# HGRN head pipeline one iteration deeper, four results taken out of PSUM by ScalarE, and two weight loads issued earlier

## The reference, cut to what matters

```python
def _hgrn2_mixer(h, w_in, lower_bound, out_norm, w_out):
    proj = h @ w_in                                   # 1024 x 1024 @ 1024 x 4096
    q, f, i, g = jnp.split(proj, 4, axis=-1)
    log_f = logaddexp(log(lb), log1p(-lb) + log_sigmoid(f))
    k  = (1.0 - lb) * sigmoid(-f)
    qf = silu(q) * HGRN_HEAD_DIM ** -0.5
    # per head: S_t = diag(f_t) S_{t-1} + k_t v_t^T ; o_t = S_t^T q_t     (v = i)
    o = scan(qf, k, i, log_f)
    o = o * rsqrt(mean(o * o, -1) + eps)              # per head
    return (o * out_norm * silu(g)) @ w_out
...
# then: x + mix, RMS norm, squared-ReLU MLP (1024 -> 4096 -> 1024), norm;
# a second block with a convolution/retention mixer and the same kind of MLP; final norm.
```

## Time and profile before

| | |
|---|---|
| time, median of 3 runs | 2488.07 us (2487.45 to 2489.05) |
| the profiled execution's own time | 2485.64 us |
| its span, first to last instruction | 2483.5 us |
| PE busy | 2437.6 us, 98% |
| DVE busy | 1049.2 us, 42% |
| ACT busy | 417.3 us, 17% |
| POOL busy | 900.4 us, 36% |
| granted TensorE clock over the span | 0.997 |

### The profile page before, as it was taken

The page is one execution under the profiler, slowest core; times in us unless marked ns, Lnnn a source line. Parts: engine busy times, 40 slices in busy tenths (PEclk is TensorE's granted clock), DMA queues, the critical chain, the costliest instruction groups (busy, mean ns, idle before and its releaser), DMA issues.

```text
span 2483.5 us, 30216 instructions
## 1 busy us (share of the span) xinstructions
PE 2437.6 (98%) x11520; PEld 2029.4 (82%) x11520; DVE 1049.2 (42%) x1449; ACT 417.3 (17%) x691; POOL 900.4 (36%) x1020
## 2 busy tenths in 40 slices
PE   7999999999999999999999999999999999999998
PEld 6888888788888888888888888888888888888886
DVE  7777777754321211211365665554421221221234
ACT  4222222222210200201230002002220110110210
POOL 3232222344333333333343333543433343343342
PEclk9999999999999999999999999999999999999999
DMA  3110101121111111111111111111111111111112
GB/s 135 35 35 26 34 25 34 50 86 59 50 44 51 51 43 50 51 48 45 51 47 63 43 34 43 43 43 51 44 50 51 51 42 51 51 44 49 51 48 79
DMA packets 36639, 123.05 MB, mean 50 GB/s; under 512 B 4704, under 2 KB 4832, under 8 KB 36576
## 3 DMA queue, kind: packets, MB, share of 16 engines
q1 hardware_dynamic: 35568, 120.54, 14.9%
q10 hardware_dynamic: 1008, 1.62, 0.2%
HBM read 117.95 MB, written 4.19 MB: 49 GB/s over the span
## 4 chain that ended last, share of the span: by engine, by line
PE 90%; DVE 5%; DVEq 3%; issue 1%; ACT 1%; DMA 0%; SPq 0%; ACTq 0%
PE prod_ps L380 28%; PE prod_ps L382 28%; PE prod_ps L381 28%; DVEq L898 2%; PE side_ps L426 2%; PE side_ps L510 1%; DVE hgrn_qk L891 1%; PE side_ps L432 1%; PE side_ps L440 1%; PE side_ps L442 1%; PE side_ps L450 1%; DVE hgrn_scores L917 1%; DVE hgrn_decay L897 1%; DVEq L921 1%; DVE x_res L1344 0%
## 5 line engine op out<-in xcount | busy, mean ns | idle before, releaser
L380 PE MATMUL prod_ps<-operand_hi,w_hi 128*128 128x512 f32 x3264 | 1286.6, 394 | 11.2 <-POOL w_lo L327 9.1
L382 PE MATMUL prod_ps<-operand_hi,w_lo 128*128 128x512 f32 x3264 | 1274.2, 390 | 0.0
L381 PE MATMUL prod_ps<-operand_lo,w_hi 128*128 128x512 f32 x3264 | 1273.2, 390 | 0.0
L323 POOL CAST w_hi<-w_raw 128x1024 fp32r<-128x1024 f32 x200 | 208.6, 1043 | 1505.8 <-PE prod_ps L382 1501.0
L380 PEld LDWEIGHTS prod_ps<-operand_hi,w_hi 128*128 128x128 f32 x3264 | 614.5, 188 | 137.8 <-POOL w_lo L327 9.1
L382 PEld LDWEIGHTS prod_ps<-operand_hi,w_lo 128*128 128x128 f32 x3264 | 614.3, 188 | 129.6
L381 PEld LDWEIGHTS prod_ps<-operand_lo,w_hi 128*128 128x128 f32 x3264 | 614.9, 188 | 123.4
L327 POOL TENSOR_TENSOR w_lo<-w_raw,w_hi 128x256 fp32r<-128x256 f32 x800 | 673.6, 872 | 16.0
L1095 DVE SCALAR_TENSOR_TENSOR work<-prod_ps,inv_rms 128x512 f32<-128x512 f32 x128 | 88.4, 692 | 492.2 <-PE prod_ps L382 491.6
L1513 ACT ACTIVATE work<-work 128x512 f32<-128x512 f32 x128 | 81.0, 633 | 1041.7 <-DVE work L1095 1041.7
L1107 DVE TENSOR_TENSOR x_res<-prod_ps,x_res 128x512 f32<-128x512 f32 x96 | 66.4, 692 | 442.6 <-PE prod_ps L382 442.6
(11 more groups left out here) (151 smaller groups left out, 1176.6 us busy)
## 6 DMA issues: line engine op xcount, KB each, us to landing
w_raw<-stream SPq DMA_DIRECT2D x204, 512.0 KB, 3.4
x_in<-x_t SPq DMA_DIRECT2D x16, 256.0 KB, 7.1
x_res<-x_t SPq DMA_DIRECT2D x8, 512.0 KB, 4.4
out_t<-x_res SPq DMA_DIRECT2D x16, 256.0 KB, 2.1
masks_f<-masks SPq DMA_DIRECT2D x1, 896.0 KB, 9.6
ret_rows<-head_rows ACTq DMA_DIRECT2D x1, 512.0 KB, 3.5
ret_cos<-rope ACTq DMA_DIRECT2D x1, 512.0 KB, 4.4
ret_sin<-rope ACTq DMA_DIRECT2D x1, 512.0 KB, 5.2
```

The costliest lines, as they stand in the source:

```text
L323: nc.gpsimd.tensor_copy(w_hi[:, slot], w_raw[:, slot]).then_inc(high_made, 1)
L380: nc.tensor.matmul(prod_ps[:, bank], w_h, a_h, start=(k == 0), stop=False)
L381: nc.tensor.matmul(prod_ps[:, bank], w_h, a_l, start=False, stop=False)
L382: last = nc.tensor.matmul(prod_ps[:, bank], w_l, a_h, start=False, stop=(k == KT - 1))
```

## The change

Five things change, all in the HGRN stage or at its border.

1. *One iteration deeper.* The units of a head come in the order v, f, q instead of q, f, v. Levels L0 to L6 of head n-1 run in iteration n, its L7 and everything behind it in iteration n+1. Scores and v get two buffers. The steps are placed so that between two levels there are mostly two half products or another step. Iterations 0 to 3 are written out, 4 to 7 are a loop of two rounds, and there are now iterations 8 and 9 beside the gate units.
2. *Four results by ScalarE.* v, k, o (as its square and a copy) and back are taken out of `side_ps` by ACT.
3. *Turn back at the end.* The turn of the normed output comes at the end of an iteration, instead of behind the turn of k.
4. *Loads.* SP's plain loop goes up to unit 31; the loop that also reloads x begins at unit 32, once the last turn back is done on PE.
5. *Smaller edits.* The two multiplies of a level become one instruction over both halves (`grown`), with 1024 instead of 512 elements a partition. `side_taken` becomes two semaphores, one for each pair of banks.

```diff
-HG_ORDER = ("L3", "L4", "L5", "L6", "L7", "v", "k", "back", "kv", "T", "o", "L0", "L1", "L2")
+HG_ORDER = ("v", "L7", "L0", "k", "L1", "kv", "L2", "T", "L3", "o", "L4", "L5", "L6", "back")
...
-            load_units(2, U_OUT1 - 2)
-            sp.wait_ge(heads_done, 1)
+            load_units(2, U_OUT1)
+            sp.wait_ge(side_done, hgrn_step(HEADS1 + 1, "back") + 1)
             for k in range(KT):
-                u = U_OUT1 - 2 + k
+                u = U_OUT1 + k
...
-                mids = [older_levels(3), older_levels(5), level7_and_v, chunk_kv, out, newer_levels(1)]
-                ends = [older_levels(4), older_levels(6), turn_k_and_back, turn_scores, after_fifth, newer_levels(2)]
+                mids = [turn_v_and_last_level, turn_k, kv_then_second_level, lambda: newer_level(3), None,
+                        lambda: newer_level(6)]
+                ends = [lambda: newer_level(0), lambda: newer_level(1), turn_scores, out_then_fourth_level,
+                        lambda: newer_level(5), back]
...
-                    nc.vector.tensor_tensor(q2[:, :, 1], q2[:, :, 1],
-                                            dec[:, :, 0:1].to_broadcast([P, pairs, h]), ALU.mult)
-                    nc.vector.tensor_tensor(k2[:, :, 0], k2[:, :, 0],
-                                            dec[:, :, 1:2].to_broadcast([P, pairs, h]), ALU.mult
-                                            ).then_inc(level_fed, 1)
+                    nc.vector.tensor_tensor(grown, grown, other, ALU.mult).then_inc(level_fed, 1)
...
+            def take_o(n):
+                step = hgrn_step(n, "o")
+                o = done_step(step)
+                nc.scalar.activation(o_sq[:], o, ACT.Square).then_inc(o_squared, 1)
+                nc.scalar.activation(o_keep[:], o, ACT.Copy).then_inc(taken(step), 1)
+            def take_back(n):
+                nc.scalar.activation(o_at, done_step(step), ACT.Copy).then_inc(taken(step), 1)
+                act.drain()
+                act.sem_inc(heads_back, 1)
...
+                if older:
+                    gather(par, n - 2, LEVELS - 1)
+                    take_v(n)
+                newer_gather(1)
...
+                newer_gather(6)
+                q_sigmoid(0)
+                q_sigmoid(1)
+                if older:
+                    take_back(n)
```

More of the change, by code:

```diff
@@ new lines, in turn_scores, with out @@
+                def turn_scores():
+                    if older:
+                        taken_from(hgrn_step(n, "L7"))
+                        turn(pair_free(hgrn_step(n, "T")), h_s[par][:].rearrange("p c t -> p (c t)"),
+                             range(1, NB, 2))
+                def out():
+                    if older:
+                        pe.wait_ge(states_ready, n - 1)
+                        taken_from(hgrn_step(n, "T"))
+                        outputs(pair_free(hgrn_step(n, "o")), h_v, h_s[par], h_state, h_q[par])
@@ L588, in _ @@
             hgrn_iteration(0, 0, mid_start=True)
-            hgrn_iteration(1, 1)
-            with pe.Fori(1, HEADS1 // 2) as i:
+            for n in range(1, 4):
+                hgrn_iteration(n, n % 2)
+            with pe.Fori(2, HEADS1 // 2) as i:
                 hgrn_iteration(i * 2, 0)
@@ L968, in hgrn_iteration @@
[L968 to L974 removed]
+                    step = hgrn_step(n, "kv")
+                    kv = done_step(step).rearrange("p (c v) -> p c v", c=NB)
                     nc.vector.tensor_copy(h_state[:, 1], kv[:, 0])
@@ L1173, in ret_states @@
                         ALU.mult, ALU.add)
-                last.then_inc(side_taken, 1)
+                last.then_inc(taken(step), 1)
                 dve.drain()
@@ new lines, in take_back, with hgrn_iteration @@
+            def take_back(n):
+                step = hgrn_step(n, "back")
+                o_at = ho[:, n - 2] if isinstance(n, int) else ho[:, bass.ds(n - 2, 1)].rearrange("p a s -> p (a s)")
+                nc.scalar.activation(o_at, done_step(step), ACT.Copy).then_inc(taken(step), 1)
+                act.drain()
+                act.sem_inc(heads_back, 1)
+            def hgrn_iteration(n, par):
+                static = isinstance(n, int)
+                newer, older = not (static and not 1 <= n <= HEADS1), not (static and not 2 <= n <= HEADS1 + 1)
@@ L1443, in hgrn_iteration, with f_sigmoids @@
-                older(4)
-                q_sigmoid(0)
-                older(5)
-                if not (isinstance(n, int) and n < 2):
-                    root(n, one_norm)
-                older(6)
-                q_sigmoid(1)
-                older(7)
-                for half in range(NH):
+                def f_sigmoids(half):
                     act.wait_ge(evac, g + (half + 3))
@@ L1490, in advance @@
+            gate_high(8)
+            take_o(HEADS1 + 1)
+            gate_sigmoid(9)
+            root(HEADS1 + 1, one_norm)
+            gate_high(9)
+            gate_sigmoid(10)
+            gate_high(10)
+            gate_sigmoid(11)
+            take_back(HEADS1 + 1)
+            gate_high(11)
+            for j in range(12, 2 * HEADS1):
+                gate_sigmoid(j)
+                gate_high(j)
             def advance(u0, make_operand, gain_row, with_gain=False):
```

469 lines of the change are left out of this document (244 added, 225 removed).

## The result

The changed kernel takes 2474.77 us (median of 4 runs, 2473.23 to 2475.37) against 2487.76 us of the kernel before in the same comparison: ratio 0.9946, 95% interval 0.9934 to 0.9959, 13.0 us faster. The forecast was 7.6 us. The profiled execution took 2474.67 us with a span of 2472.8, against 2485.64 and 2483.5: 10.7 us of span.

The account below looks back on a forecast made before the run. PE, busy 98% of the span, was taken as the bound, so only its waits could be won: 33.2 us in the HGRN stage before, 25.6 after, gain 7.6, so 2488.07 - 7.6 = 2480 us; eight-in-ten range 2469 to 2488.

Parts of the forecast that it names:

- L7 waits once per iteration: Sign in PE's timeline: a level waits for its gather only behind the turn of v, by 2 to 3 us.
- The merged multiply: One DVE multiply of 1024 elements per level reads 1.22 us and gains nothing, -0.06 us a level.
- The waits before: PE's waits in the HGRN stage of the old kernel, counted as 33.2 us.
- The waits after: PE's waits in the HGRN stage of the changed kernel, forecast as 25.6 us.
- L2 and T: In a full iteration, L2 waits 0.4 us for L1's scores and T 0.2 us for the states.
- Iteration 8: Beside the gate units, waits of 6.8 us: L7 2.4, T 2.3, back 0.9, L6 0.5, L2 0.4, small 0.3.
- ScalarE's copies: Results taken from PSUM by ACT, 1.06 us assumed; only back's moves the sum, DVE's 4.9 us relief lies off the path.
- The loads: Units 30 and 31 no longer wait for the heads and unit 32's load is covered: nothing.
- Branches: Loop branches cost about 0.5 us each, on ACT ahead of L7's gather in two iterations: 1.0 us.
- L7's wait mostly absent: Rival: DVE's chain after L5 is 2 us shorter, six waits shrink, 13 us more gained, 2467; chance 0.15.
- the gain eaten: Rival: chain after L5 1 us longer, or wait instructions cost PE 0.1 each; 5.4 us lost, 2486; chance 0.25.
- a lower rate of the merged multiply: Rival: the multiply takes 2.44 us instead of 1.22, making the kernel slower, 2507; chance 0.12.

Follow-up runs that it names:

- e3_split: The changed kernel with each level's merged multiply made two multiplies of 512 elements again: 2488.91 us.
- e6_tail: e4_early with iteration 8 reordered: states, T and norm ahead of gate steps on DVE, back ahead of the sixth gate sigmoid on ScalarE: 2461.48 us.
- e10_back: The changed kernel with back alone taken out of PSUM by DVE again, v, k and o staying with ScalarE: 2466.25 us.
- e2_dve_takes: The changed kernel with v, k, o and back all taken out of PSUM by DVE again: 2467.49 us.
- e11_vko: The changed kernel with v, k and o taken out by DVE again and back still by ScalarE: 2476.66 us.
- e7_loads: The changed kernel with the loads of units 30 and 31 issued behind the last turn back again: 2484.26 us (median of nine runs).
- e5_unrolled: The changed kernel with all eight head iterations written out instead of a loop for the last four: 2470.97 us.
- e4_early: The changed kernel with ScalarE's gather for L7 and copy of back moved ahead of the second sigmoid of q: 2463.20 us.

## Why the prediction was right, and where it was not

The sign and the main place of the waits that remain, L7, were right, and 2474.8 us lies in the range of 2469 to 2488; the gain was 5.4 us larger than said, and two terms were priced wrongly on the way. Of its signs, L7 waits once per iteration, but by 0.7 to 1.9 us and not 2 to 3, and the period is 49.8 to 51.2 us and not 51.5 to 52.2. The merged multiply reads 1.22 to 1.23 us, L0 of head 0 does not wait, and T of iteration 8 waits 2.3, as said.

*The waits before* were 33.2 us by my count. Summed over all starts of the stage, less the pitch of each kind of matmul, they are 34.5: right. This level hangs on the pitch taken (there are some 1750 product matmuls, so 0.003 us more or less on each moves it by 5 us); the difference between two kernels does not.

*The waits after* were to be 25.6 us and are 20.1 by the same sum, of which 15.9 in waits of over 0.12 us and 1.0 of slow clock among them.
- L7 waits in every iteration from 3 to 8, as forecast, 8.4 us and not 6 x 2.3 = 13.8. Count from the end of L5: in iteration 3 the chain takes 11.7 us and not 13.2. The collision of level L6 with POOL (0.5) and the one at the multiply by the sigmoid (0.5) did not fall there, and the copy took 1.01 and not 1.06; the rest is some 0.3 us less from L5 to the norm. In the loop the chain takes 12.55: one of the collisions is back (L964) and there are the gaps of the loop.
- L2 and T do not wait at all where I had 0.4 + 0.2 each time, some 3.5 us in all. L1's multiply took 1.27 us beside POOL where I had 1.15 and its share of two collisions; e3_split shows that the wait at L2 (0.51) is real with two multiplies.
- Iteration 8: T 2.26 (2.3 forecast) and back 0.67 (0.9) are right; L2 and L6 wait nothing.
- Iteration 9: L7 waits 3.34 us, and I had 0.7 for the whole iteration. I had walked DVE's queue there and not ScalarE's: back's copy, whose bank L7 needs, stands behind the sixth gate sigmoid. e6_tail shows it: with the copy ahead, that wait is gone.
- The start: no wait at L0, as forecast.

*Where the gain comes from* was wrong. "The merged multiply: nothing, -0.06 a level" is the step that failed. The size of one multiply is exactly as said (1.22 to 1.23 us free), but I compared it with two multiplies in the quiet, where the walk itself charged 0.54 per instruction beside POOL; two instructions pay twice. So it is at L1 (1.89 us for 1.27, and L2's wait of 0.51 seven times). At L7 even the 0.07 a level that I counted are worth more than themselves: without that saving DVE's small multiply falls behind POOL's cast and pays 0.9 (e3_split). The merge is worth 10.4 us in the old order, 9.4 in the new with DVE's copies and 14.1 with ScalarE's. The rule that I cited for a price per instruction gives what L1 shows, and I did not apply it to this term. I also read the rows against full blocking, because POOL's four subtractions and DVE's multiplies went on together: they are four instructions, and singly they and DVE's take turns (e3_split). That the forecast came out near in spite of this is in part luck: the walk after the change had one collision for L6's multiply in it, which is right for the merged form alone: e3_split, the same walk without the merge, waits 37.8 us.

*ScalarE's copies* were priced at nothing against DVE's, and this failed too. The copy of back was in my chain at 1.06, but not the comparison: on DVE it lies beside the sigmoid and costs the chain nothing. e10_back puts this at 8.5 us, e2_dve_takes at 7.3. "DVE is freed of 4.9 us per iteration, off the path" was right: e11_vko is 1.9 us from the change, inside the runs' scatter.

*The loads* were priced at nothing, and nothing is late. What I did not say is that the deeper order needs this edit: its last turn back ends where unit 30 begins (494.82), and without it the time is 9.5 us longer (e7_loads).

*Branches* were 1.0 us and cost L7 3.0 in iterations 5 to 7 (e5_unrolled), because the delay brings a collision with it. What they cost in all stays open.

*The clock.* I had no term for it, and I read the page as the upper level all through. A digit there is a mean over 62 us; a stretch of 6.8 us at the lower clock, at 1328.3 in the trace before, does not show in it. In the trace after, it takes back 1.0 us at 456 and 3.1 at the norms.

The rivals: L7's wait mostly absent did not come in this kernel (e4_early is what it would have been, 2463, and I had 2467); the gain eaten is e3_split's case; a lower rate of the merged multiply is refuted by its rows, 1.23 and 1.34 us.

## What to carry to other kernels

Price an edit against the chain that ends last and beside what runs there, not by its duration in the quiet: one multiply for two saved 0.07 us where POOL was idle, 0.6 where POOL was at work, 0.9 where a delay of tenths let another instruction fall behind POOL's cast, and between 4 and 14 us of the kernel by how much slack the chain had. When work goes to the emptier engine, ask what it then stands in front of in that engine's queue; here 1.01 us of copy between a sigmoid and a gather cost 8.5 us. And when a wait stays, look first at which ready instruction stands behind one that waits for something else: moving such instructions in iteration ends and in iteration 8 gave 17.7 us, more than the change itself.

## What was not expected of the hardware

- POOL's cast can hold back a DVE multiply until it ends, even one of 16 elements (0.17 alone, 1.05 held; it ends at 391.95, the cast at 391.91). One that starts with the cast pays nothing, one that starts 0.13 us or more behind always does, and in between, at 0.08 to 0.09, 7 of 34 do. A larger multiply that starts shortly before the cast's end pays about 0.13 (0.69 to 0.81, 1.22 to 1.34). POOL's four subtractions let DVE in between them, in turns, at some 0.54 an instruction (0.69 to 1.23), and each turn lengthens a subtraction as well (0.73 to 1.19).
- ScalarE reads 1024 elements a partition from PSUM in 1.01 us, no slower than from SBUF (1.06).
- In the head stage of these kernels, 18 of 29 waits of PE of 2.0 us or more were followed by a stretch at the lower clock, and none of the some 130 between 0.35 and 1.94 us was. Waits of the same length did both (of seven between 2.24 and 2.26 us three were followed by a stretch and four were not). A stretch makes mostly four to nine product matmuls 0.2 us longer each, so a wait of 2.3 us can cost 3 to 4 (an estimate from these counts).
